# Turning the feed-forward norms' input through the DMA queue instead of TensorE, and taking the first two feed-forward chunks tile by tile

## The reference

```python
x = x + 0.5 * _swiglu(_rms_norm(x, ffn1_norm[l]), w_gate, w_up, w_down)     # D_FF = 2816
h = _rms_norm(x, mix_norm[l])                                               # the mixer:
y = gates[:, :, 0] * y_conv + gates[:, :, 1] * y_mla                        #  convolution and attention branch
x = x + y @ w_out[l]
x = x + 0.5 * _swiglu(_rms_norm(x, ffn2_norm[l]), w_gate, w_up, w_down)
# _swiglu(h) = (silu(h @ w_gate) * (h @ w_up)) @ w_down
```

## Time and profile before

| | us |
|---|---|
| median of 3 runs | 1050.41 (1050.13 to 1051.11) |
| profiled execution | 1050.95 |
| its span in the profile | 1049.1 |
| PE busy in the span | 1043.1 (99%) |
| PEld busy | 874.6 (83%) |
| DVE busy | 682.4 (65%) |
| ACT busy | 586.6 (56%) |
| POOL busy | 247.3 (24%) |

### The profile page before, as it was taken

How to read it: one execution, slowest core, us unless ns; L and a number is a source line. 1 busy time by engine, 2 the same in 40 slices (tenths; PEclk the granted TensorE clock), 3 DMA queues, 4 the chain that set the end, 5 groups by cost and what they waited for, 6 DMA issues and landing times.

```text
span 1049.1 us, 13803 instructions
## 1 busy us (share of the span) xinstructions
PE 1043.1 (99%) x5025; PEld 874.6 (83%) x5025; DVE 682.4 (65%) x905; ACT 586.6 (56%) x786; POOL 247.3 (24%) x258
## 2 busy tenths in 40 slices
PE   9999999999999999999999999999999999999998
PEld 6888888998888888888888888889988888888887
DVE  6755654798977666555467555646989666656551
ACT  6754544576873764445366454536778547645440
POOL 2960000148850000000048300002588300000000
PEclk9999999999999999999999999999999999999999
DMA  8978566555555496675469667565366366976641
GB/s 281 307 236 237 183 210 200 145 197 174 208 170 154 147 311 189 205 235 195 129 177 294 214 209 228 184 194 172 124 209 223 118 181 195 273 224 183 207 140 41
DMA packets 185219, 207.24 MB, mean 198 GB/s; under 512 B 57776, under 2 KB 156368, under 8 KB 185168
## 3 DMA queue, kind: packets, MB, share of 16 engines
q1 hardware_dynamic: 183952, 204.45, 63.4%
q10 hardware_dynamic: 1216, 2.11, 0.9%
HBM read 192.90 MB, written 1.05 MB: 185 GB/s over the span
## 4 chain that ended last, share of the span: by engine, by line
PE 97%; ACT 1%; DVE 1%; DMA 0%; issue 0%; POOL 0%; ACTq 0%
PE bank L641 30%; PE bank L643 30%; PE bank L642 30%; PE bank L722 1%; PE bank L680 1%; PE bank L885 1%; PE bank L894 1%; PE bank L915 1%; PE bank L648 1%; DMA qkT<-qkT 0%; PE bank L893 0%; PE bank L917 0%; DVE htok L1508 0%; DVE x L1556 0%; ACT htok L1112 0%; PE bank L903 0%
## 5 line engine op out<-in xcount | busy, mean ns | idle before, releaser
L1481 DVE TENSOR_TENSOR wlo<-raw,whi 128x2048 fp32r<-128x2048 f32 (+2 forms) x152 | 347.5, 2289 | 86.1 <-ACT whi L1103 85.1
L641 PE MATMUL bank<-whi,hThi 128*128 128x512 f32 (+1 forms) x976 | 378.6, 388 | 0.0
L643 PE MATMUL bank<-whi,hTlo 128*128 128x512 f32 (+1 forms) x976 | 373.7, 383 | 0.0
L642 PE MATMUL bank<-wlo,hThi 128*128 128x512 f32 (+1 forms) x976 | 373.5, 383 | 0.0
L1103 ACT ACTIVATE whi<-raw 128x2048 fp32r<-128x2048 f32 (+2 forms) x176 | 335.4, 1911 | 23.1 <-DMA raw<-in_ffn_w_up 11.3
L643 PEld LDWEIGHTS bank<-whi,hTlo 128*128 128x128 f32 x976 | 183.2, 188 | 35.9
L641 PEld LDWEIGHTS bank<-whi,hThi 128*128 128x128 f32 x976 | 183.3, 188 | 35.1 <-issue 0.3
L642 PEld LDWEIGHTS bank<-wlo,hThi 128*128 128x128 f32 x976 | 183.4, 188 | 34.6
L1185 ACT ACTIVATE gates<-bank,small 128x256 f32<-128x256 f32 x88 | 41.8, 475 | 265.8 <-PE bank L643 265.2
L641 PE MATMUL bank<-whi,gThi 128*128 128x512 f32 (+1 forms) x416 | 162.1, 390 | 0.0
L643 PE MATMUL bank<-whi,gTlo 128*128 128x512 f32 (+1 forms) x416 | 161.1, 387 | 0.0
(11 more groups left out here) (171 smaller groups left out, 818.1 us busy)
## 6 DMA issues: line engine op xcount, KB each, us to landing
raw<-in_ffn_w_down SPq DMA_DIRECT2D x88, 512.0 KB, 4.3
raw<-in_ffn_w_gate SPq DMA_DIRECT2D x84, 512.0 KB, 4.5
raw<-in_ffn_w_up SPq DMA_DIRECT2D x84, 512.0 KB, 5.6
raw<-in_w_in SPq DMA_DIRECT2D x48, 512.0 KB, 4.9
raw<-in_w_out SPq DMA_DIRECT2D x16, 512.0 KB, 4.3
raw<-in_w_in SPq DMA_DIRECT2D x8, 544.0 KB, 4.4
raw<-in_w_mla_out SPq DMA_DIRECT2D x8, 512.0 KB, 3.9
raw<-in_w_conv_out SPq DMA_DIRECT2D x8, 512.0 KB, 4.9
```

Source lines behind the costliest of these rows:

```text
L641: nc.tensor.matmul(out, lh, rh, start=start, stop=False, skip_group_check=skip)
L642: nc.tensor.matmul(out, lh, rl, start=False, stop=False, skip_group_check=skip)
L643: return nc.tensor.matmul(out, ll, rh, start=False, stop=stop, skip_group_check=skip)
L1481: nc.vector.tensor_tensor(wlo[:, slot(u0, RING), 0:n], raw[:, slot(u0, RAW), 0:n], whi[:, slot(u0, RING), 0:n].bitcast(F32), ALU.subtract) ...
```

## The change

For the three feed-forward norms other than the very first (second block of layer 0, first of layer 1, second of layer 1), `x` is turned by the block path: ACT `x_split` (2 `block_split`), SP `norm_turn` (2 DMA transposes), DVE `x_join` (2 `block_join`), ACT `block_gained` (8 instructions, reading SBUF instead of PSUM) and DVE `block_gained_rest` (8). PE no longer turns them. PE takes chunks 0 and 1 tile by tile: (chunk 0, tile 0), (1, 0), (0, 1), (1, 1). ACT and DVE split units 2 and 3 ahead of tile 1's turn. In the mixer, DVE's first residual (tile 0) moves ahead of its last steps on `y`. The blocks' serial numbers (`nth`) are counted from a list. The core of the diff:

```diff
@@ SP, ffn @@
                     if (l, f, c) != (0, 0, 1):
                         gate_up(l, f, c, c, 0)
+                        if c == 1 and f == 1:
+                            norm_turn(l, 2, 0)
+                        if c == 2 and (l, f) != (0, 0):
+                            norm_turn(l, 2 * f, 1)
                         gate_up(l, f, c, c, 1)
+                        if c == 1 and f == 0:
+                            norm_turn(l, 0, 0)
@@ PE, ffn first, last, mixer @@
-                        gate_up(0, 0, 0, between=lambda: norm(l, n, 1))
-                        gate_up(0, 0, 1)
                         for t in range(TT):
-                            gate_up(1, 1, t)
+                            for c in range(2):
+                                gate_up(c, c, t)
...
-                        if (t, f) == (1, 1) and l + 1 < DEPTH:
-                            norm(l + 1, 0, 0)
...
-                         between={0: lambda: second_tile(0), 2: lambda: second_tile(1), 3: lambda: norm(l, 2, 0)})
+                         between={0: lambda: second_tile(0), 2: lambda: second_tile(1)})
@@ ACT @@
+            def x_split(l, n, t):
+                act.wait_ge(x_new, l * 6 + (n * TT + t + 1))
+                for h in range(2):
+                    block_split(nth_norm(l, n, t), h, x[:, t, h * 512:(h + 1) * 512])
+            def block_gained(l, n, t):
+                for h in range(2):
+                    act.wait_ge(block_joined[h], nth_norm(l, n, t) + 1)
+                    for k in range(4):
+                        ins = nc.scalar.activation(hThi[:, 4 * h + k, t * P:(t + 1) * P],
+                                                   block_out[h][:, k * P:(k + 1) * P], ACT.Copy,
+                                                   scale=fgain[:, n // 2, l, 4 * h + k:4 * h + k + 1])
+                    ins.then_inc(nhi, 1)
@@ ACT, ffn first @@
-                    split(l, UB[f] + 2)
                     silu(0, 0)
+                    block_gained(l, 2 * f, 1)
                     norm_squares(l, 2 * f, 1)
-                    split(l, UB[f] + 3)
                     split_planes(0, 0)
                     silu(0, 1)
                     split(l, UB[f] + 4)
@@ ACT, last chunk, after split(*after) @@
+                if f == 1 and not final:
+                    x_split(l + 1, 0, 0)
+                    norm_squares(l + 1, 0, 0)
@@ ACT, between the mixer and the second block @@
-                ffn_norm(l, 2, 0)
-                ffn_rounds(l, 2, 1)
+                x_split(l, 2, 0)
+                norm_squares(l, 2, 0)
+                block_gained(l, 2, 0)
+                split(l, UB[1] + 2)
+                split(l, UB[1] + 3)
+                x_split(l, 2, 1)
                 ffn(l, 1)
@@ DVE, end of the mixer @@
                 for h in range(2):
-                    block_join(l * 2 + 1, h)
+                    block_join(nth("y", l), h)
+                    if h == 1:
+                        residual(l, 1, 0, 4, UM + U_MIX - 1)
                     dve.wait_ge(yt_hi, l * 4 + 3 + h)
                     block_rest(h, 1).then_inc(yt_lo, 1)
-                    if h == 0:
-                        one()
+                one()
                 one()
@@ DVE, between the mixer and the second block @@
-                residual(l, 1, 0, 4, UM + U_MIX - 1)
-                rest_of(2, 0)
+                norm_scale(l, 2, 0)
+                x_join(l, 2, 0, yt_lo, l * 4 + 3)
+                block_gained_rest(l, 2, 0)
                 residual(l, 1, 1, 2, UM + U_MIX - 1)
-                norm_scale(l, 2, 0)
-                rest_of(2, 1)
+                split(l, UB[1] + 2)
+                split(l, UB[1] + 3)
+                x_join(l, 2, 1, nlo, per_norm_half(l, 2, 0, 0))
+                block_gained_rest(l, 2, 1)
                 ffn(l, 1)
```

More of the change, by code:

```diff
@@ L65 @@
 M_PR, M_C01, M_UQ, M_UKV, M_C23, M_G, M_MLA, M_CO, M_WO = 0, 2, 4, 5, 6, 8, 16, 18, 20
+BLOCKS = [(what, l) for l in range(DEPTH) for what in ("first0", "first1", "mix", "y", "second0", "second1")
+          if l or not what.startswith("first")]
 USED = [2048] * U_LAYER
@@ L103, in unit_down, with nth, nth_norm @@
     return c * 3 + (UB[f] + 6)
+def nth(what, l):
+    return BLOCKS.index((what, l))
+def nth_norm(l, n, t):
+    return nth(f"{'second' if n else 'first'}{t}", l)
 def two_pi_parts(value, quanta):
@@ L331, in per_turned @@
                 return h * TT + t + 1
-            return l * 10 + (0, 2, 6)[n] + t * 2 + h + 1
+            return 2 * TT + 2 * l + h + 1
         def norm_bank(l, n, t, h):
@@ L395, in block_turn, with norm_turn @@
                 sp.dma_start_transpose(block_turned[h][:, :, :], block_words[h].bitcast(U16)).then_inc(block_landed[h], 16)
+            def norm_turn(l, n, t):
+                for h in range(2):
+                    block_turn(nth_norm(l, n, t), h)
             def x_half(t, h, landed):
@@ L433, in first @@
                             for h in range(2):
-                                block_turn(l * 2 + 1, h)
+                                block_turn(nth("y", l), h)
                 first()
@@ L473, in _ @@
                 for h in range(2):
-                    block_turn(l * 2, h)
+                    block_turn(nth("mix", l), h)
                 block_of(l, UM + M_UQ, a["w_uq"], 0, 2, 0, H * QK)
@@ L1145, in factors @@
                                      ACT.Copy).then_inc(fgain_ready, 1)
[L1147 to L1155, removed]
             def block_split(g, h, words):
@@ L1263, in ffn @@
                     act.wait_ge(h_ready, l * TT + 1)
-                    block_split(l * 2, 0, htok[:, 0:512])
+                    block_split(nth("mix", l), 0, htok[:, 0:512])
                 silu(c, 1)
                 if f == 0:
-                    block_split(l * 2, 1, htok[:, 512:1024])
+                    block_split(nth("mix", l), 1, htok[:, 512:1024])
                 elif not final:
@@ L1440, in mixer @@
                     act.wait_ge(y_ready, l * 4 + 3 + h)
-                    block_split(l * 2 + 1, h, gates[:, 1, h * C:(h + 1) * C])
+                    block_split(nth("y", l), h, gates[:, 1, h * C:(h + 1) * C])
                 one()
                 for h in range(2):
-                    block_round(l * 2 + 1, h, 1, yt_hi)
+                    block_round(nth("y", l), h, 1, yt_hi)
                 assert next(s) == UB[1] + 2
@@ L1459, in _ @@
                 else:
-                    ffn_norm(l, 0, 0)
-                    ffn_rounds(l, 0, 1)
+                    block_gained(l, 0, 0)
+                    split(l, UB[0] + 2)
+                    split(l, UB[0] + 3)
+                    x_split(l, 0, 1)
                 ffn(l, 0)
                 for h in range(2):
-                    block_round(l * 2, h, 0, nhi)
+                    block_round(nth("mix", l), h, 0, nhi)
                 norm_squares(l, 1, 1)
@@ L1497, in block_rest, with x_join, block_gained_rest @@
                             hThi[:, 4 * h:4 * h + 4, t * P:(t + 1) * P])
+            def x_join(l, n, t, read, count):
+                for h in range(2):
+                    dve.wait_ge(read, count + h)
+                    block_join(nth_norm(l, n, t), h)
+            def block_gained_rest(l, n, t):
+                for h in range(2):
+                    dve.wait_ge(nhi, per_norm_half(l, n, t, h))
+                    for k in range(4):
+                        o = hTlo[:, 4 * h + k, t * P:(t + 1) * P]
+                        ins = nc.vector.scalar_tensor_tensor(out=o, in0=block_out[h][:, k * P:(k + 1) * P],
+                                                             scalar=fgain[:, n // 2, l, 4 * h + k:4 * h + k + 1],
+                                                             in1=hThi[:, 4 * h + k, t * P:(t + 1) * P].bitcast(F32),
+                                                             op0=ALU.mult, op1=ALU.subtract)
+                    ins.then_inc(nlo, 1)
             def norm_scale(l, n, t):
@@ L1632, in ffn @@
                 mul(c, 1)
+                if f == 1 and not final:
+                    x_join(l + 1, 0, 0, nlo, per_norm_half(l, 2, 1, 0))
                 if not final:
@@ L1868, in _ @@
             for l in range(DEPTH):
-                def rest_of(n, t):
-                    for h in range(2):
-                        gained_rest(l, n, t, h)
                 if l == 0:
@@ L1881, in _ @@
                 else:
-                    rest_of(0, 0)
+                    block_gained_rest(l, 0, 0)
                     residual(l - 1, 2, 1, 2, UB[1] + U_FFN - 1)
                     norm_scale(l, 0, 0)
-                    rest_of(0, 1)
+                    split(l, UB[0] + 2)
+                    split(l, UB[0] + 3)
+                    x_join(l, 0, 1, nlo, per_norm_half(l, 0, 0, 0))
+                    block_gained_rest(l, 0, 1)
                 ffn(l, 0)
                 for h in range(2):
-                    block_join(l * 2, h)
+                    block_join(nth("mix", l), h)
```

## The result

| | median us | runs | span of the profiled execution |
|---|---|---|---|
| before | 1050.38 (1050.13 to 1051.11) | 6 | 1049.1 |
| changed | 1056.08 (1052.34 to 1056.23) | 6 | 1054.2 |

What follows compares the result with a forecast made beforehand. PE was taken as the bound, busy 1043.1 of 1049.1 us. Per block -1.79 for transposes removed and +2.25 for a new wait give +0.46, three blocks +1.4: median 1050.41 to 1051.8, range 1049.3 to 1055.0.

Steps and rivals of the forecast that it cites:

- The slots of the turns: PE's 48 transposes on `x`, six turns: each turn removed gives PE back 0.89 us, 5.3 us in all.
- 83% of it: Share of weight loads on PE by a skill's rule; if only that came back, 5.3 us would be 4.4.
- Tile 0 in time: Turn of tile 0 by DMA ends at 343.7 and 344.8, before PE asks at 345.15; margin 1.4 us, no stall.
- Tile 1 in time: Turn of tile 1 ends at 354.6 and 355.8, before PE asks at 356.0 and 358.8; margin again 1.4 us.
- The new wait at chunk 2: Before `gate_up(2, tile 0)`, PE waits 2.25 us for `mul(1, 0)`, behind units 4 and 5, in each of three blocks.
- Rival (b): At `gate_up(0, tile 1)`, tile 1's turn is late too, 4.8 us more, 1056.6; chance 0.15 with latenesses of its kind.
- rival (d): After the 2.25 us waits the clock falls to 1.2 GHz over 24 matmuls, at worst three times: +16, 1068; chance 0.02.

Runs made afterwards that it cites:

- The control with the weaker wait in the kernel before: Kernel before, with only chunk 2's first gate/up piece waiting for chunk 0's product instead of chunk 1's: 1050.14 us, ratio 0.9997.
- the run with one wait: Changed kernel, chunk 2 waiting for chunk 0's product in two of three blocks, the old wait kept in layer 0's second block: 1046.62 us, ratio 0.9967.

## Why the prediction was wrong

1. **The slots of the turns**, 0.89 each, 5.3 in all: right. Each of the six turns gives back 0.87 to 0.90 us, by the starts of the matmuls around it before and after, and so the full slot and not 83% of it. With every wait gone the profiled span is 1043.0 against 1049.1, and 0.95 of those 6.1 belongs to point 5.
2. **Tile 0 in time**: right. Its last half (`block_gained_rest`) ended in the changed kernel at 344.8 as worked out, and no PE wait for `hTlo` is left. The trace gives a margin of 1.2 where 1.4 was worked out, and the run with the late residual shows that it is needed: the residual goes from 334.19 to 338.32, 4.1 later, and PE waits 1.86.
3. **Tile 1 in time**: right. Worked out 354.6 and 355.8 for the two halves, traced 354.8 and 356.1. The old order shows what the new one is for: without it PE waits 4.1 a block. Rival (b) fell: no wait for `hTlo` is there. That its price, 1056.6, lies so near the measured 1056.1 is chance.
4. **The new wait at chunk 2**: right in place, cause and size. Worked out 2.25, traced 2.25 (2.14 and 0.11), three times. (A sum beside it is 0.1 off: with a wait of 2.0 the time is 1050.41 + 3 x 0.21 = 1051.0, not 1051.1.)
5. **Missed, small and on the other side**: PE's wait for `htok` at the mixer's norm of layer 1, 1.1 us in the earlier trace rows, is gone; by the starts of the matmuls there (1.34 us apart before, 0.39 after) that is 0.95. In the trace of before, a transpose just ahead of it took 4.9 us to land and held DVE's list; in the changed kernel it landed in time. The control with the weaker wait in the kernel before has the 1.1 too. Why the transpose is slower there wasn't tested.
6. **The step that failed: rival (d), the clock**, given 0.02 and priced at up to 16. The sum put the clock at nothing: it took the wait at its length and let PE go on at full speed, since the clock had held through 1.05 us, and no row had 2 us. The clock did fall, in the profiled execution three times, 0.8 to 1.2 us after the restart, and cost 1.6 us each, +4.8. The one row spoke for idle times up to its own length and for no longer one; read as evidence for 2.25 it was carried twice as far as it reaches. The price was too high as well, because it assumed a whole piece of 24 matmuls at 1.2 GHz where 8 went so. The Trainium skill, "TensorE: Matmul & The Clock Gate", § What's actually happening, says that the default is throttled and that the engine's recent activity releases the clock; these runs agree, as matmuls of zeros in the wait kept it at 0.999 to 1.0 and took 4.3 us off (3.6 by the ratios). That the fall comes in one execution and not in the next at the same wait is shown by the run with one wait (two of six).

Without the clock the sum would have been -5.3 - 0.95 + 6.75 = +0.5: the +1.4 that was forecast, less point 5. The two versions with zeros put in, at +0.8 and +1.0 over their medians of before, lie there.

## What to carry to other kernels

When work goes off the bounding engine, look not only at whether its substitute is in time, but at what the reordering puts last in the in-order lists of the helpers: here two lists stood still for 4 to 5 us with ready work behind a wait, and then PE stood still. A wait on the wrong, later product is free as long as it is early; check which buffer it protects before an order is changed. And a stall of TensorE of about 2 us costs nearly twice its length, when the clock falls after it; a microsecond didn't.

## What the runs showed of the hardware

- After idle times of 2.0 us on PE (2.4 between weight loads) the granted clock fell to 0.5, in four traced cases 0.3 to 1.2 us after the restart and for 8 matmuls, in some executions and not in others. After 0.8 to 1.0 us it stayed, in 15 runs (six and nine) with three such waits each. In the old order's waits of 3.56 to 4.35 us it had fallen in all three blocks by the time PE went on (0.66 in 355 to 360):

```profile
355.00:360.00 5.00, 4.63 (x14) 3.70 (x14) 1.91 (x8) 2.12 (x5) 0.56 (x1) 0.66 0.80 289
```

- A fall hardly shows in PE's busy share: 99% before and after, with none and with three.
- The block transposes took 3.1 to 4.6 us to land in the changed kernel, 3.2 in the median, in all 20.
